# Attention A's units placed among block 1's projections, the output product in two halves by rows, and the rope addition on GpSimd

## The reference

```
x = concat([meta(16 rows), x])                       # 272 keys
h = rms_norm(x, attn_norm_g); proj = h @ w_in
qa, ka, va, qb, kb, vb = split(proj, [512,128,128,512,512,512])
# A: 8 query heads of 64 on 2 key/value heads
qa, ka = rope(rms_norm(qa)), rope(rms_norm(ka))
out_a = softmax(qa @ ka.T / 8) @ va
# B: 4 heads, each two softmax maps of 64-wide queries and keys
qb, kb = rope(rms_norm(qb)), rope(rms_norm(kb))
w = p0 - lam * p1
out_b = rms_norm(w @ vb, subln_g) * (1 - lam_init)
x = x + concat([out_a, out_b]) @ w_out               # 1024 x 1024
h = rms_norm(x, ffn_norm_g)
x = x + (silu(h @ w_gate) * (h @ w_up)) @ w_down
```

## Time and profile before

| what | value |
|---|---|
| median of 3 runs | 800.71 us (799.9 to 804.59) |
| profiled execution, its own time | 800.42 us |
| its span from first to last instruction | 799.1 us |
| busy in the span: PE, DVE, ACT, POOL | 96%, 58%, 47%, 13% |
| matmuls and loads, DVE, ACT, POOL instructions | 4442 each, 651, 540, 121 |
| memory read | 127.96 MB, 161 GB/s over the span |

### The profile page before, as it was taken

The page is one execution under the profiler, slowest core; times in us unless marked ns, Lnnn a source line. Parts: engine busy times, 40 slices in busy tenths (PEclk is TensorE's granted clock), DMA queues, the critical chain, the costliest instruction groups (busy, mean ns, idle before and its releaser), DMA issues.

```text
span 799.1 us, 10991 instructions
## 1 busy us (share of the span) xinstructions
PE 763.8 (96%) x4442; PEld 665.1 (83%) x4442; DVE 465.2 (58%) x651; ACT 373.2 (47%) x540; POOL 102.1 (13%) x121
## 2 busy tenths in 40 slices
PE   6979789999999999999999999999988999999997
PEld 5867678799999999978888888887867999888895
DVE  5788535366555555556575666574586655444433
ACT  6544573265344444354352534474255554444431
POOL 1496232020000000004000000000200110111110
PEclk9999797999999999999999999999999999999999
DMA  9533204378656666615744545145472775655521
GB/s 338 173 87 114 68 30 130 110 252 262 186 183 186 186 184 187 184 54 175 231 160 154 180 151 193 41 142 179 161 227 67 239 240 192 184 184 187 181 65 53
DMA packets 71043, 129.79 MB, mean 162 GB/s; under 512 B 5281, under 2 KB 29041, under 8 KB 70993
## 3 DMA queue, kind: packets, MB, share of 16 engines
q1 hardware_dynamic: 69376, 125.45, 49.2%
q0 software_dynamic: 1408, 3.54, 1.3%
q10 hardware_dynamic: 208, 0.10, 0.0%
HBM read 127.96 MB, written 1.05 MB: 161 GB/s over the span
## 4 chain that ended last, share of the span: by engine, by line
PE 89%; DVE 4%; POOL 4%; ACT 1%; issue 1%; DMA 1%; SPq 0%; DVEq 0%; ACTq 0%; POOLq 0%
PE psum L403 46%; PE psum L672 27%; PE psum L456 3%; PE psum L691 2%; PE psum L534 2%; PE psum L602 1%; PE psum L792 1%; PE psum L732 1%; PE psum L578 1%; PE psum L480 1%; PE psum L434 1%; POOL head_square_sums L1687 1%; PE psum L471 1%; POOL vb_meta L1734 1%; DVE tmp L1628 1%
## 5 line engine op out<-in xcount | busy, mean ns | idle before, releaser
L1178 DVE TENSOR_TENSOR w_lo<-w_raw,w_hi 128x1024 fp32r<-128x1024 f32 x223 | 271.2, 1240 | 153.5 <-ACT w_hi L839 152.4
L839 ACT ACTIVATE w_hi<-w_raw 128x1024 fp32r<-128x1024 f32 x231 | 237.0, 1061 | 149.6 <-PE psum L672 80.8
L672 PE MATMUL psum<-h_hi,w_hi 128*128 128x256 f32 x608 | 172.7, 284 | 2.2 <-DVE h_lo L1191 1.7
L672 PE MATMUL psum<-h_hi,w_lo 128*128 128x256 f32 x608 | 171.9, 283 | 0.0
L672 PE MATMUL psum<-h_lo,w_hi 128*128 128x256 f32 x608 | 171.0, 281 | 0.0
L403 PE MATMUL psum<-w_hi,h_hi 128*128 128x512 f32 (+1 forms) x352 | 140.5, 399 | 12.6 <-DVE w_lo L1272 7.0
L403 PE MATMUL psum<-w_hi,h_lo 128*128 128x512 f32 (+1 forms) x352 | 137.8, 392 | 0.0
L403 PE MATMUL psum<-w_lo,h_hi 128*128 128x512 f32 (+1 forms) x352 | 137.8, 391 | 0.0
L672 PEld LDWEIGHTS psum<-h_hi,w_hi 128*128 128x128 f32 x608 | 114.7, 189 | 3.5 <-issue 2.8
L672 PEld LDWEIGHTS psum<-h_lo,w_hi 128*128 128x128 f32 x608 | 115.0, 189 | 0.7
L672 PEld LDWEIGHTS psum<-h_hi,w_lo 128*128 128x128 f32 x608 | 114.4, 188 | 0.0
(11 more groups left out here) (289 smaller groups left out, 956.3 us busy)
## 6 DMA issues: line engine op xcount, KB each, us to landing
w_raw<-in_w_in SPq DMA_DIRECT2D x78, 512.0 KB, 4.7
w_raw<-in_w_down SPq DMA_DIRECT2D x54, 512.0 KB, 4.3
w_raw<-in_w_up SPq DMA_DIRECT2D x32, 512.0 KB, 4.4
w_raw<-in_w_gate SPq DMA_DIRECT2D x44, 256.0 KB, 2.9
w_raw<-in_w_up SPq DMA_DIRECT2D x44, 256.0 KB, 3.2
w_raw<-in_w_out SPq DMA_DIRECT2D x16, 512.0 KB, 4.2
w_raw<-in_w_branch_a SPq DMA_DIRECT2D x4, 512.0 KB, 5.2
w_raw<-in_w_branch_b SPq DMA_DIRECT2D x4, 512.0 KB, 5.0
```

The costliest lines, as they stand in the source:

```text
L672: mm = pe.matmul(outs, x[:, cols], y[:, kc, :], start=kc == 0 and n == 0, stop=kc == KC - 1 and n == 2)
L839: act.activation(T.w_hi[:, k % SLOTS, :], T.w_raw[:, k % RAW_SLOTS, :], ACT.Copy).then_inc(S.w_rounded, 1)
L1178: dve.tensor_tensor(T.w_lo[:, k % SLOTS, :], T.w_raw[:, k % RAW_SLOTS, :], T.w_hi[:, k % SLOTS, :], ALU.subtract).then_inc(S.w_cut, 1)
```

## The change

Attention A goes first. The slabs now come as qa, kva, qb, kb, vb. The last three are cut into pieces (`piece(name, n_pass, j)`: two chunks of the weights for one tile, six matmuls of 512 columns; pass 2 is the meta rows with four), and the output product into 32 pieces of three matmuls (`out_piece`): first the upper half of its rows (`oa`, attention A's) with all four sums, then the lower half (`ob`, attention B's), each added to `x` by itself (8 additions, 4 before). Between the pieces stand A's scores, transposes and products, then B's. All five engines' orders are written out step by step, and the scores' banks are 0 and 1, then 7, 0, 1.

In the rope, the sum of the two table products is moved from VectorE (6 instructions of 512 columns, 2 of 128) to GpSimd (`add_turned`). Of the output product's fills GpSimd now makes the remainders of 4, not 6. `pT`, the turned maps, has memory of its own in place of `rope_part`'s; `meta_stack` is 48 columns wide in place of 128. The transposes of x for the feed-forward part are split: the left half among the last pieces, the right half behind the first quarter of the feed-forward's first product.

The diff, cut to its core (fills 18 to 21 are `oa`, 22 to 25 `ob`, 26 to 29 the first of the feed-forward part):

```diff
-        for name in ("qb", "kb", "kva", "qa", "vb"):
+        for name in ("qa", "kva", "qb", "kb", "vb"):
...
-        self.by_pool = set(range(f["out", 0], f["out", 0] + 6))
+        self.by_pool = {f["oa", 0] + 1, f["oa", 0] + 3, f["ob", 0] + 1, f["ob", 0] + 3}
...
+SCORE_BANK = (0, 1) * 8 + (0, 1) * 4 + (7, 0, 1, 7, 0, 1, 7, 0)
+SCORE_FREE = [max([m + 1 for m in range(n) if SCORE_BANK[m] == SCORE_BANK[n]], default=0) for n in range(32)]
+MAP_BANK, SUMS = 2, {"a": (3, 6), "b": (4, 5)}
...
+PASSES = {name: ((0, 0, 4), (1, 0, 5)) for name in ("qb", "kb", "vb")}
+PASSES["oa"] = ((0, 0, 3), (1, 0, 6), (0, 1, 3), (1, 1, 6))
+PASSES["ob"] = ((0, 0, 0), (1, 0, 1), (0, 1, 2), (1, 1, 3))
...
+    def piece(name, n_pass, j):
+        k, passes = W.first[name] + j, PASSES[name]
+        if j == 0 and name != "qb" and n_pass < 2:
+            pe.wait_ge(S.products, {"kb": 5, "vb": 7}[name] + n_pass)
+            pe.wait_ge(S.rope_squared, {"kb": 6, "vb": 8}[name] + n_pass)
+        if j == 0 and n_pass == 2:
+            pe.wait_ge(S.heads_cut, HEADS["qb"] + 2 if name == "kb" else HEADS["kb"] + 3)
+        if n_pass == 0:
+            pe.wait_ge(*W.cut(S, k))
...
+    def out_piece(name, n_pass, j):
...
+        if n_pass == 0:
+            pe.wait_ge(*W.cut(S, k))
+            pe.wait_ge(S.cut_done, CUT["mixa" if name == "oa" else "mixb"] + j // 2 + 1)
...
+    slab("qa", KC, ((0,), (1,)), first=True)
+    slab("kva", KC, ((2,), (3,)), meta=7)
...
+    turn_ka()
+    piece("kb", 0, 0)
+    piece("kb", 0, 1)
+    turn_kam()
+    piece("kb", 1, 0)
+    piece("kb", 1, 1)
+    scores(0)
+    scores(1)
+    piece("kb", 0, 2)
...
-        dve.tensor_tensor(dst, dst, part, ALU.add).then_inc(S.rotated, 1)
...
+    def add_turned(name, t, dst):
+        pool.wait_ge(S.products, 2 * (ROTATED[name] - 1) + t + 1)
+        pool.tensor_tensor(dst, dst, T.part[:, t, 0:dst.shape[1]], ALU.add).then_inc(S.rotated, 1)
```

More of the change, by code:

```diff
@@ L438, in slab, with by_chunk, slab_by_bank @@
                 between[j, per - 1]()
-    def slab_by_bank(name, chunks, banks, x_hi=T.h_hi, x_lo=T.h_lo, ready=None, free=None, order=None):
+    def by_chunk(n, last, w_hi, w_lo, x_hi, x_lo, kc, t, out):
+        for i, (x, y) in enumerate(((x_hi, w_hi), (x_hi, w_lo), (x_lo, w_hi))):
+            mm = pe.matmul(out, x[:, kc, t * P:(t + 1) * P], y, start=n == 0 and i == 0, stop=last and i == 2)
+        return mm
+    def slab_by_bank(name, chunks, banks, x_hi=T.h_hi, x_lo=T.h_lo, ready=None, free=None):
         per, k0 = W.per[name], W.first[name]
@@ L536, in scores @@
         mm.then_inc(S.scored, 1)
[L538 to L552 removed]
     def open_sums(kind):
         for b in SUMS[kind]:
[L558 removed]
+            pe.matmul(bank[b][:], T.zero[:], T.qT["a"][:, 0:2, :], start=True, stop=False)
     def turn_unit(u):
@@ new lines, in tensor_program @@
+    scores(5)
+    turn_qb(1)
+    turn_unit(1)
+    scores(6)
+    attend_unit(0)
+    piece("kb", 1, 3)
+    scores(7)
+    piece("vb", 0, 0)
+    scores(8)
+    attend_unit(1)
+    turn_unit(2)
+    piece("kb", 2, 0)
+    scores(9)
+    piece("kb", 2, 1)
+    scores(10)
+    turn_unit(3)
+    piece("kb", 2, 2)
+    piece("kb", 2, 3)
+    scores(11)
+    attend_unit(2)
+    scores(12)
+    piece("vb", 1, 0)
+    turn_unit(4)
+    attend_unit(3)
+    piece("vb", 0, 1)
+    turn_kb(0)
+    turn_unit(5)
@@ new lines, in tensor_program @@
+    scores(13)
+    piece("vb", 0, 2)
+    attend_unit(4)
+    scores(14)
+    turn_kb(1)
+    piece("vb", 0, 3)
+    scores(15)
+    piece("vb", 1, 1)
+    turn_unit(6)
+    turn_kbm()
+    piece("vb", 1, 2)
+    scores(16)
+    attend_unit(5)
+    scores(17)
+    piece("vb", 2, 0)
+    scores(18)
+    turn_unit(7)
+    scores(19)
+    piece("vb", 2, 1)
+    piece("vb", 2, 2)
+    scores(20)
+    scores(21)
+    attend_unit(6)
+    piece("vb", 2, 3)
+    turn_unit(8)
+    attend_unit(7)
+    scores(22)
@@ new lines, in tensor_program @@
+    attend_unit(8)
+    scores(23)
+    scores(24)
+    piece("vb", 1, 3)
+    turn_mixa()
+    turn_unit(9)
+    scores(25)
+    scores(26)
+    scores(27)
+    turn_unit(10)
+    out_piece("oa", 0, 0)
+    out_piece("oa", 0, 1)
+    scores(28)
+    scores(29)
+    out_piece("oa", 0, 2)
+    scores(30)
+    scores(31)
+    attend_unit(9)
+    attend_unit(10)
+    turn_unit(11)
+    out_piece("oa", 1, 0)
+    out_piece("oa", 0, 3)
+    turn_unit(12)
+    attend_unit(11)
+    turn_unit(13)
+    attend_unit(12)
@@ new lines, in scalar_program @@
+    round_fill(20)
+    exp1(13)
+    round_kb(1)
+    exp_lam()
+    exp1(14)
+    take_vb0()
+    exp1(15)
+    round_kbm()
+    round_fill(21)
+    copy_unit(6)
+    exp1(16)
+    exp1(17)
+    copy_unit(7)
+    exp1(18)
+    exp1(19)
+    round_fill(22)
+    exp1(20)
+    copy_unit(8)
+    copy_vb_meta()
+    exp1(21)
+    exp1(22)
+    round_fill(23)
+    exp1(23)
+    exp1(24)
+    round_mixa(0)
+    copy_unit(9)
+    round_mixa(1)
+    exp1(25)
+    exp1(26)
+    exp1(27)
+    exp1(28)
+    copy_unit(10)
@@ L1342, in vector_program @@
+    head_sum("ka", 1)
+    cut_fill(9)
+    scale_qa(0)
+    scale_qa(1)
+    rows_ka(0)
+    rows_ka(1)
+    head_sum("kam", 0)
+    cut_fill(10)
+    scale_ka(0)
+    scale_ka(1)
+    rows_qb(0)
+    cut_fill(11)
+    head_sum("qb", 0)
+    cut_qa(0)
+    rows_qb(1)
+    head_sum("qb", 1)
+    cut_qa(1)
+    cut_ka()
+    cut_kam()
+    cut_fill(12)
     max1(0)
+    multiply_lam()
     max1(1)
-    rotate("qa", 1, bank[3][:], qb[1])
+    scale_qb(0)
     max1(2)
+    scale_qb(1)
+    cut_fill(13)
@@ L1366, in gather @@
[L1366 to L1371 removed]
     max1(6)
+    rows_kb(0)
+    cut_fill(15)
     max1(7)
[L1375 to L1379 removed]
@@ L1425, in add_residual @@
+    dens_b()
+    sum_squares(0)
+    sum_squares(1)
+    add_out("oa", 1)
+    scale_b(0)
+    scale_b(1)
+    cut_mixb(0)
+    add_out("oa", 2)
+    cut_mixb(1)
+    cut_fill(26)
+    add_out("oa", 3)
+    add_out("ob", 0)
+    add_out("ob", 1)
+    add_out("ob", 2)
+    cut_h2(0)
+    cut_h2(1)
+    add_out("ob", 3)
+    cut_fill(27)
+    mean_rows(1)
+    cut_fill(28)
+    cut_fill(29)
+    cut_h2(2)
+    cut_h2(3)
+    def add_residual(half, dones, banks, scales):
         for t in range(TILES):
```

1171 lines of the change are left out of this document (722 added, 449 removed).

## The result

The changed kernel takes 793.33 us (median of 8 runs, 791.19 to 798.29), the kernel before took 802.46 beside it (8 runs, 799.9 to 805.5). The ratio is 0.990, with an interval of 0.987 to 0.993: faster, by 9 us where the prediction had 19, and outside its range of 776 to 791. The profiled execution took 793.73 us with a span of 792.4.

What follows compares the result with a forecast made beforehand. TensorE, busy for 96% of the span, bounds the kernel, so only its waits and lowered clock can be won: 23.2 us less 4.2 left (0.7 + 0.5 + 2.0 + 1.0) gives 19.0, so 800.4 becomes 781.4 us, range 776 to 791.

Steps and rivals of the forecast that it cites:

- 0.7 of the start: At the start, TensorE waits for late remainders of h that chunk 4 needs: 0.7 us, bounds 0 and 2.5.
- 0.5 of ka's meta rows: Before A's first scores, TensorE waits for GpSimd's chain for ka's meta rows: 0.5 us, bounds 0 and 2.5.
- 2.0 of holds: From 40 to 60 us, GpSimd and VectorE hold each other up: 2.0 us, bounds 0 and 7.7.
- 1.0 of hops: Small hops of a hundred written handovers between engines: 1.0 us, bounds 0 and 3.
- The chain of kb's meta rows: Ahead of B, GpSimd's longest new chain, 13.4 us, is covered by 14.7 us of TensorE's work.
- Both falls of the earlier trace: In the kernel before, half-clock stretches at 90 to 100 and 120 to 130 us, together 8.2 us to be won.
- from the feed-forward to the end the span is as before, within 1 us: From the feed-forward part to the kernel's end, the change was to leave the time as it was.
- The ceiling: Most that can be won: 14.05 us idle, 8.2 of clock and 0.9 of a feed-forward input wait, 23.2 us.
- The clock still falls: Likeliest at B's units between last scores and output product, one or two clock falls: 785 to 790 us, chance 0.15.
- GpSimd the bound up to 60 us: Up to 60 us, GpSimd's work makes qa, ka, kam and qb each 2 us late: about 788 us, chance 0.11.
- The waits only move: Single late steps in the in-order lists bring back half of the 23.2 us: 789 to 793 us, chance 0.10.
- Slower by a total exclusion: Up to the feed-forward, VectorE stands still during all GpSimd tensor operations, 44 us: 809 us, chance 0.04.

Runs made afterwards that it cites:

- a3_gpsimd_remainders_apart: Changed kernel with GpSimd's remainders of fills 21 and 23 moved apart, each behind a weighed map of B: 787.94 us, ratio 0.981.
- b1_all_three: Changed kernel with block 2's constants late, VectorE's remainders of fills 27 to 29 early and GpSimd's remainders of 21 and 23 apart: 781.26 us, ratio 0.972.
- the upper group: Six of the unedited changed kernel's 14 runs, at 797.0 to 798.3 us with a mean granted clock of 0.984 to 0.986.
- a1_constants_late: Changed kernel with GpSimd's eight loads of block 2's constants moved behind the feed-forward's fifth step, the second row scale's root ahead of them: 785.69 us, ratio 0.979.
- the lower group: Eight of the unedited changed kernel's 14 runs, at 791.0 to 793.7 us (median 792.4) with a mean granted clock of 0.992 to 0.994.
- b2_remainders_one_by_one: Changed kernel with GpSimd's remainder of fill 21 in place and that of fill 23 waiting for head 1's weighed map: 789.17 us, ratio 0.982.

## Why the prediction was wrong

**The idle time up to the feed-forward: right in sum, wrong in its parts.** I left 4.2 us of idle time. TensorE idled from 7.20 to 145.56 us for 4.1 (160 - 147.15 = 12.85, less 7.20 at the start and the 1.57 from 158.43 to 160). But it isn't 0.7 of the start, 0.5 of ka's meta rows, 2.0 of holds and 1.0 of hops. The start cost nothing behind the first matmul, ka's rows 0.3, hops about nothing, and holds 3.7. One hold of 4.1 us (4.31 - 0.22) near 104 us gave a single wait of 3.2, over the 2.5 that I had named as a sign of being wrong. I had put the hold of VectorE before 60 us, as a loss of 1.4 us. One did come there and cost 0.5: beside GpSimd's addition at 32.13 us (1.29 us) a weight remainder of VectorE that starts at 32.15 takes 2.35 us in place of 1.21 and ends at 34.50, and TensorE goes on at 34.56:

```profile
32.13 1.29 POOL L2259 TENSOR_TENSOR tmp<-tmp,rope_part 128x512 f32<-128x512 f32 x1
```

```profile
32.15 2.35 DVE L1498 TENSOR_TENSOR w_lo<-w_raw,w_hi 128x1024 fp32r<-128x1024 f32 x1
```

The additions were held in turn: one that starts at 26.64, just behind a remainder of VectorE from 26.48 (1.22 us), takes 2.20 us, and one behind a remainder from 60.28 takes 2.19, both over the 2 us that I had named as a sign too. TensorE waited for neither.

**The start of the feed-forward** I gave as 141 us. That is a slip: the terms ahead of it give 160.5 - 14.05 - 8.2 + 4.2 = 142.4, as the last 0.9 us was counted behind it. It was 145.56. The price of the rival *GpSimd* is a slip as well: 8 us in place of 3.2 give 786, not 788.

**The chain of kb's meta rows** held, as said: TensorE came to their transposes at 86.87 us without a wait.

**The clock.** Both falls of the earlier trace rows are gone, worth the 8.2 us. But the hole of 3.2 us made a new one, which I had as a rival at 0.15 and not in the sum. Without any fall TensorE's work up to the feed-forward takes 131.9 (`a3_gpsimd_remainders_apart`: 139.52 less 7.61 idle) to 132.7 us (`b1_all_three`); in the profile after it takes 145.56 - 7.20 - 4.1 = 134.3. So the fall cost 1.6 to 2.4 us there, and some 4 more in the profile of the upper group. The new order's own work is 0.6 to 1.4 us above the 131.3 that my count of before had left (160.49 - 6.97 - 14.05 - 8.2).

**The step that failed is "from the feed-forward to the end the span is as before, within 1 us".** From the first product of the feed-forward to the end the kernel before took 799.1 - 160.49 = 638.6 us, the changed one 792.4 - 145.56 = 646.8: 8.2 more. Of these 5.62 - 0.56 = 5.1 are the wait for VectorE's copy behind the remainders of fills 31 to 33. Another 2.0 are the lower clock that follows: the 96 matmuls of the second step take 13.68 us, where they take 11.64 in `a1_constants_late` and 11.63 before. And 0.9 are the transposes of the right half of x (0.87 us at 148.57), which before all stood ahead of the feed-forward's first product: the change itself moved them behind it, and the prediction left that out. The prediction listed what each moved instruction waits for on SyncE's queue and GpSimd's at the start, and not at the end: VectorE's remainders of fills 27 to 29 stand behind the additions to x, GpSimd's constants hang on the output product's last fill, and the small copy that opens the second step stands behind the bulk remainders in VectorE's list. With these loads moved alone, 7.5 of the 8.2 came back (`a1_constants_late`: 783.8 - 144.45 = 639.35 us); what stays is about the transposes.

**A misreading** of 0.9 us: I took the second wait of the earlier trace rows for the feed-forward's input to stand behind 160.5 us and counted it as won. It stands in block 2; in `b1_all_three` it is at 592.18 us, still 0.90. The ceiling was 22.3 us, not 23.2.

The errors add up to the difference: 0.2 for a later start, -0.1 idle time, 3.0 of work and clock, 8.2 behind the feed-forward's start and 0.9 misread make 12.2, and the span is 792.4 where the forecast had 780.1.

**The rivals.** *The clock still falls* named B's units and the reciprocal, product and two passes on VectorE as its place, and that is where it fell; its price of 6.1 us, waits included, lies between what the lower group loses against `a3_gpsimd_remainders_apart` (792.4 - 787.9 = 4.5) and what the upper one does (9.6). It gave 785 to 790, since it had one loss and there were two. *GpSimd the bound up to 60 us* did not come: GpSimd's six additions have a median of 1.32 us, and TensorE was busy for 51.91 of 53 us from 7 to 60. *The waits only move* gave 789 to 793 for half the gain coming back, which is nearest in size; it had no place for it. *Slower by a total exclusion* did not come.

**The Trainium skill**, "SBUF — State Buffer", section "Who interferes with whom", had the rule that acts in the first hole: a VectorE instruction with two inputs in SBUF and a GpSimd instruction that reads SBUF exclude each other. The trace agrees where one GpSimd instruction ran (2.01 us for a 0.22 us product in `b2_remainders_one_by_one`, 2.35 for a 1.21 us remainder at 32.15 us). With two back to back the product was held through both, 4.31 us, which I had not reckoned with. I had weighed the rule only for the additions that the change adds, and 5.7 us by it for those was far too much: the one hold by an addition that reached TensorE cost it 0.5 us. It acted on an instruction that was there before, with 2 elements a partition, and on remainders that were there before, when the new order put them side by side.

## What to carry to other kernels

When a change makes one stage earlier, list everything that is tied to that stage's end, above all bulk loads on another queue, and everything that is tied to its own engine's list; what was 5 us apart and 15 us early may now meet. Look above all for a small step that TensorE waits for and that stands behind bulk work in another engine's list. The profile may call that wait "issue": the kernel's own waits name the semaphore. Read the order across engines for short two-input VectorE instructions on the path beside long GpSimd ones, more than for long beside long: the short one paid 4.1 us here and a long one 1.1, of which 3.2 and 0.5 reached TensorE. Count a hole of TensorE with the clock behind it: here 0.9 us cost about its length, and 3.2 us cost its length, another 1.6 to 2.4 in one profile and some 4 more in another. Compare kernels within 1% run by run with their mean granted clocks, not by medians alone.

## What the runs showed of the hardware

- Two GpSimd tensor operations issued without a gap held VectorE's 128x2 product for both: 4.31 us, against 2.01 with a semaphore wait between them and 0.22 with none beside it. The kernels differ in that wait alone for the first two figures.
- After the same hole of 3.2 us the granted clock from 110 to 120 us was 0.83, 0.90 or 0.50 from one profile of nearly the same instructions to the next, and the medians of the two groups of runs, which differ in mean clock, lie 5.1 us apart. After 0.9 us it stayed at 1.00. What decides between them stays open.
- With the transfer engines full (share 1.01, 335 GB/s), the six transfers of 256 KB for fills 31 to 33 took 8.0 to 10.7 us from issue to landing. With the constants gone from the stretch (`a1_constants_late`, second line) the same six took 2.7 to 4.7:

```profile
DMA to landing us min/median/max: 8.0/10.0/10.7
```

```profile
DMA to landing us min/median/max: 2.7/3.8/4.7
```
